# First down projection of a two-block kernel: each product as two of 64 rows into two banks

## What is computed

```python
def conv_ffn(x, g_norm, w_up, conv_k, conv_b, w_down):
    h = rms_norm(x, g_norm)
    up = h @ w_up
    ...
    gate, val = jnp.split(up, 2, axis=-1)
    return x + (jax.nn.silu(gate) * val) @ w_down
```

## Time and profile before

| | |
|---|---|
| Median of three runs | 2355.01 us (2355.0 to 2355.7) |
| Span of the profiled execution | 2353.4 us |
| What the runs' median has beside the profiled span | 1.6 us |
| TensorE busy | 2343.1 us, 12,183 products and as many weight loads |
| VectorE busy | 1516.3 us |
| ScalarE busy | 1223.8 us |
| DMA | 432.66 MB, mean 184 GB/s |
| Mean granted TensorE clock | 1.000 |

### The profile page before, as it was taken

The page is one execution under the profiler, slowest core; times in us unless marked ns, Lnnn a source line. Parts: engine busy times, 40 slices in busy tenths (PEclk is TensorE's granted clock), DMA queues, the critical chain, the costliest instruction groups (busy, mean ns, idle before and its releaser), DMA issues.

```text
span 2353.4 us, 35087 instructions
## 1 busy us (share of the span) xinstructions
PE 2343.1 (100%) x12183; PEld 1963.4 (83%) x12183; DVE 1516.3 (64%) x2146; ACT 1223.8 (52%) x1931; POOL 68.7 (3%) x92
## 2 busy tenths in 40 slices
PE   9999999999999999999999999999999999999999
PEld 7887788888888888888888878888887888888887
DVE  5657655556577775477776668787876755555554
ACT  5445544444465554355554475756465455555543
POOL 0011200000200000000000000000000000000000
PEclk9999999999999999999999999999999999999999
DMA  8665555565656656566655655555554575656555
GB/s 272 219 207 178 171 190 190 180 200 185 222 179 196 193 183 199 182 196 188 194 184 189 192 154 169 153 169 151 161 149 148 180 223 163 193 155 187 169 169 171
DMA packets 289497, 432.66 MB, mean 184 GB/s; under 512 B 32976, under 2 KB 129136, under 8 KB 289264
## 3 DMA queue, kind: packets, MB, share of 16 engines
q1 hardware_dynamic: 282976, 422.69, 57.6%
q10 hardware_dynamic: 6416, 8.56, 1.1%
HBM read 429.07 MB, written 7.10 MB: 185 GB/s over the span
## 4 chain that ended last, share of the span: by engine, by line
PE 95%; DVE 2%; ACT 1%; DVEq 1%; issue 0%; DMA 0%; ACTq 0%
PE gemm L559 22%; PE gemm L561 22%; PE gemm L560 22%; PE gemm L544 7%; PE aux L544 7%; PE gemm L537 3%; PE aux L537 3%; PE aux L1939 2%; DVE w_lo L504 1%; PE aux L561 1%; PE aux L560 1%; PE aux L559 1%; ACT w_hi L494 1%; PE aux L2180 0%; PE aux L2399 0%; PE aux L2380 0%
## 5 line engine op out<-in xcount | busy, mean ns | idle before, releaser
L504 DVE TENSOR_TENSOR w_lo<-raw,w_hi 128x1024 fp32r<-128x1024 f32 (+1 forms) x800 | 958.1, 1206 | 572.3 <-ACT w_hi L494 567.4
L494 ACT ACTIVATE w_hi<-raw 128x1024 fp32r<-128x1024 f32 (+1 forms) x800 | 815.6, 1042 | 506.0 <-PE gemm L561 402.7
L559 PE MATMUL gemm<-w_lo,hT 128*128 128x512 f32 x1600 | 637.0, 398 | 0.7 <-DVE hT L1224 0.6
L561 PE MATMUL gemm<-w_hi,hT 128*128 128x512 f32 x1600 | 624.0, 390 | 0.0
L560 PE MATMUL gemm<-w_hi,hT 128*128 128x512 f32 x1600 | 623.3, 390 | 0.0
L559 PEld LDWEIGHTS gemm<-w_lo,hT 128*128 128x128 f32 x1600 | 300.6, 188 | 64.8 <-issue 4.1
L561 PEld LDWEIGHTS gemm<-w_hi,hT 128*128 128x128 f32 x1600 | 300.3, 188 | 63.8
L560 PEld LDWEIGHTS gemm<-w_hi,hT 128*128 128x128 f32 x1600 | 300.8, 188 | 58.8 <-issue 0.2
L544 PE MATMUL gemm<-hT,w_hi 128*128 128x512 f32 x704 | 218.5, 393 | 0.1
L544 PE MATMUL aux<-hT,w_hi 128*128 128x512 f32 x672 | 208.0, 390 | 0.0
L559 PE MATMUL gemm<-w_lo,yT_hi 128*128 128x512 f32 x472 | 184.3, 390 | 0.5 <-DVE yT_lo L1467 0.5
(11 more groups left out here) (341 smaller groups left out, 2283.4 us busy)
## 6 DMA issues: line engine op xcount, KB each, us to landing
raw<-in_w_up SPq DMA_DIRECT2D x336, 256.0 KB, 2.9
raw<-in_w_in SPq DMA_DIRECT2D x144, 512.0 KB, 4.4
raw<-in_a_w_in SPq DMA_DIRECT2D x128, 512.0 KB, 3.6
raw<-in_b_w_in SPq DMA_DIRECT2D x128, 512.0 KB, 4.2
raw<-in_w_down SPq DMA_DIRECT2D x76, 512.0 KB, 4.6
raw<-in_w_branch SPq DMA_DIRECT2D x32, 512.0 KB, 4.5
raw<-in_w_out SPq DMA_DIRECT2D x32, 512.0 KB, 4.7
raw<-in_a_w_out SPq DMA_DIRECT2D x32, 512.0 KB, 3.7
```

What stands on the lines that cost most here:

```text
L494: nc.scalar.activation(hi, src, ACT.Copy).then_inc(S("hi_done"), 1)
L504: nc.vector.tensor_tensor(lo, src, hi.bitcast(F32), ALU.subtract).then_inc(S("lo_done"), 1)
L559: nc.tensor.matmul(dst, xh, wl[:, k, :], start=h["start"] and k == 0, stop=False)
L561: mm = nc.tensor.matmul(dst, xl, wh[:, k, :], start=False, stop=h["stop"] and k == h["n"] - 1)
```

## The change

For tiles 41 to 44, each of the three products of a k block and token block is done as two: the lower 64 rows of both operands into the tile's `G` bank, the upper 64 rows into the `AX` bank with the number `t % 2 * 2 + tb`. Both banks hold half of the sum over the rows. The three terms now stand in one loop, each with its two halves. At the end of such a tile VectorE first adds the `AX` bank to `x`, drains, and then adds the `G` bank; the signal to TensorE comes from the second. All other tiles are as before.

```diff
--- before.py
+++ after.py
@@ -508,6 +508,14 @@
 
             return T_UP1 <= t < T_DOWN1 or T_UP2 <= t < T_DOWN2
 
+        def in_row_halves(t):
+
+            return T_DOWN1 <= t < T_UP2
+
+        def half_banks(t, tb):
+
+            return G[t % 2][tb], AX[t % 2 * 2 + tb]
+
         def up_banks(t):
 
             return G[t % 2] + AX[t % 2 * 2:t % 2 * 2 + 2]
@@ -552,7 +560,16 @@
             order = [(k, tb) for k in range(h["n"]) for tb in range(TB)]
             if t == N_TILES - 1 and h["stop"]:
                 order.sort(key=lambda at: at[1])
-            for k, tb in () if is_up(t) else order:
+            if in_row_halves(t):
+                for k, tb in order:
+                    at = slice(tb * P, (tb + 1) * P)
+                    terms = ((hi, wl), (hi, wh), (lo, wh))
+                    for i, (xs, ws) in enumerate(terms):
+                        for rows_, dst in zip((slice(0, C), slice(C, P)), half_banks(t, tb)):
+                            mm = nc.tensor.matmul(dst[:, 0:w], xs[rows_, h["kt"] + k, at], ws[rows_, k, :],
+                                                  start=h["start"] and k == 0 and i == 0,
+                                                  stop=h["stop"] and k == h["n"] - 1 and i == 2)
+            for k, tb in () if is_up(t) or in_row_halves(t) else order:
                 xh = hi[:, h["kt"] + k, tb * P:(tb + 1) * P]
                 xl = lo[:, h["kt"] + k, tb * P:(tb + 1) * P]
                 dst = (AX[tb] if t in IN_AUX else G[t % 2][tb])[:, 0:w]
@@ -1423,6 +1440,9 @@
                 for tb in range(TB):
                     dst = x[:, tb, bass.ds(at, 512)]
                     src = AX[tb] if t in IN_AUX else G[t % 2][tb]
+                    if in_row_halves(t):
+                        V.tensor_tensor(dst, dst, half_banks(t, tb)[1][:, :], ALU.add)
+                        dve.drain()
                     V.tensor_tensor(dst, dst, src[:, :], ALU.add).then_inc(S(f"read_out{tb}"), 1)
 
             run(half, 8, turn_merged(3))
```

## The result

The change takes 2360.72 us (median of 11 runs, 2359.81 to 2361.11) against 2355.15 for the kernel before (11 runs): a ratio of 1.0023, 95% interval 1.0015 to 1.0031. That is 5.6 us slower; 2360.9 was predicted, 5.9 over before.

What follows compares the result with a forecast made beforehand. TensorE's stream was taken to bound the kernel, with VectorE costing only where TensorE waits. Joints 5.5, mode changes 0.4 and products 0 gave 5.9 us over the median 2355.0: 2360.9, range 2355.5 to 2366.5.

Steps and rivals of the forecast that it cites:

- The adds at the joints: Between a tile's end and the third half's w_lo, VectorE's doubled adds cost 1.52 us at each of three places, 4.56 us.
- The products: In the first down projection, each pair of 64-row products costs what one undivided product did, 226.7 ns: 0 added.
- the fp32 pace: Rival for the divided products: pairs run at 0.216 us each, -5.6 us, giving 2355.8, no change; chance 0.20.
- the whole product's pace: For the divided products: 226.7 ns per pair, as for one undivided fp32r product of 512 columns.
- The remainder of fp32r: About 13 ns beyond streaming in each fp32r product; forecast: a pair pays it together; the fp32 pace has it vanish.
- The second start: Rival: each pair of divided products pays 0.01 us for its second product's start, 5.3 us, giving 2365.7; chance 0.12.
- Entering and leaving: TensorE's one switch into 64-row mode costs 0.19 us and the one out 0.20, together 0.4.
- The fourth joint: After the last divided tile, at the second up projection's first tile, the adds cost 0.99 us after slack.
- Nothing else queues behind the adds: On VectorE after the adds: raw tile loads follow w_lo, issued four halves ahead; the bank's next writer is two tiles away.
- The sum: Over the whole kernel: 5.5 + 0.4 + 0 = 5.9 us, added to the median 2355.0: 2360.9, or 0.25% more.
- The likeliest case: The forecast itself for the whole kernel, 2360.9 us, reaching from 2359.7 to 2362.3 with its unknown adds; chance 0.55.

Runs made afterwards that it cites:

- adds-only run: Kernel before, with each bank of the first down projection added twice to x, a drain between, and products undivided: 2360.16 us, ratio 1.0021.
- third half first: VectorE splits the next tile's third weight half before waiting for the tile's end: 2354.39 us on the change, 2354.74 on the kernel before.
- pairs-only run: The change without the second add, so products are divided but VectorE adds only the gemm bank: 2355.74 us, ratio 1.0004 to the kernel before.
- the runs with many changes: The change for token block 0 only: 2393.06 us; the same with each half's products sorted by token block: 2376.41 us.
- third half first with the products of before: Kernel before, with VectorE splitting the next tile's third weight half before it waits for the tile's end: 2354.74 us, ratio 0.9998.
- halves far apart: The change, with all lower-row products of a half of the weights before all upper-row ones: 2475.59 and 2443.45 us in two runs.

## Why the prediction was right

*The adds at the joints: right.* Forecast 1.52 at each of three, by two adds and two drains; measured 4.6 us in all in the waits, and 1.57 a tile with the slower restart. The mechanism is shown twice: the adds-only run alone loses 5.0, and with the third half first it is all gone. Only the form was other than said: the chain has no product of 1.8 us, it leaves TensorE and goes through the adds.

*The products: right, for 0.* The choice between the fp32 pace and the whole product's pace fell to the second, and the pairs run every 0.23 us like the products of the earlier trace rows. The remainder of fp32r stays when two products share the array. Had it gone, the pairs-only run would have been 4 to 5 us below before and not 0.6 above. The second start is not paid: the two of a pair start 0.00 to 0.01 us apart, and the next pair is not later for it. The Trainium skill's rule was that each further tile of a pack adds some 4 ns (the Trainium skill, "TensorE: Matmul & The Clock Gate", section "Measured speedup vs the span model"). Across this stream of pairs that does not add up: by an estimate from this figure it would be 2.1 us, and the pairs-only run loses 0.5 in the whole stage, with both changes of mode.

*Entering and leaving: right*, 0.4. In the runs with many changes it is 0.43 to 0.44 for there and back.

*The fourth joint: right for the adds by themselves, too high for the change.* Forecast 0.99, and 0.20 beside it for leaving the mode. How late TensorE is against the kernel before can be read from the starts of the same products ahead of this joint (988.95 before) and behind it (990.35 before). With the adds alone they are 994.66 and 997.04: from 5.71 to 6.69, so 0.98, as forecast. In the change they are 994.19 and 996.37: from 5.24 to 6.02, so 0.78. Leaving the mode has made TensorE 0.2 later already, and that much less is left to wait for. The forecast added two terms that overlap.

"Nothing else queues behind the adds" is not borne out either. Later, at 1004.8, TensorE waits again. Before, there was a stall at the same place:

```profile
998.51 0.30 PEld L544 LDWEIGHTS gemm<-hT,w_hi 128*128 128x128 f32 x2 [0.48 <-issue]
```

and after:

```profile
1002.36 1.06 ACT L494 ACTIVATE w_hi<-raw 128x1024 fp32r<-128x1024 f32 x1 [1.87 <-DMA raw<-in_w_up]
...
1004.79 0.30 PEld L552 LDWEIGHTS gemm<-hT,w_hi 128*128 128x128 f32 x2 [0.74 <-issue]
```

At the head of the second up tile w_lo is late because w_hi waited for the load of the raw tile (1.87 us, the row at 1002.36), and that load may start only when w_lo has freed the raw tile. The chain of the change runs this way, from the adds by w_lo, SyncE and the load to the product at 1004.82: a delay of VectorE can come back by way of SyncE four halves later. Here it is 0.26 us more than before. But VectorE's delay alone does not set it. The adds-only run has the same adds and waits only 0.2 us at this place, and the pairs-only run, whose joints are the old ones, does not wait there at all; nor do the two runs with the third half first. What else decides, the time of the load perhaps, stays open.

*The sum: the number owes something to luck.* By the starts of the same products in the two profiled executions the change is 0.12 us late ahead of the stage (866.82 against 866.70), 5.24 behind it, 6.02 behind the fourth joint and 6.27 behind the stall at 1004.8 (1005.82 against 999.55). So the stage and its tail cost 6.15, not the 5.9 of the forecast: three times 1.57 and 0.4 for the mode, then 0.78 and 0.26. The spans differ by only 5.6, because two later stalls, far behind the change, are shorter in it by 0.37 us each. The first of them, before:

```profile
1236.02 0.69 DVE L1462 TENSOR_TENSOR conv_val<-conv_gate,conv_val 128x512 f32<-128x512 f32 x1 [0.46 <-issue]
...
1240.24 0.19 PEld L559 LDWEIGHTS gemm<-w_lo,yT_hi 128*128 128x128 f32 x1 [0.90 <-DVE yT_lo L1467]
```

and after:

```profile
1241.92 0.69 DVE L1482 TENSOR_TENSOR conv_val<-conv_gate,conv_val 128x512 f32<-128x512 f32 x1
...
1246.14 0.19 PEld L576 LDWEIGHTS gemm<-w_lo,yT_hi 128*128 128x128 f32 x1 [0.53 <-DVE yT_lo L1487]
```

Before, VectorE stands still for 0.46 us and waits for nothing that the profile shows; after, it does not, and TensorE is stopped for 0.37 us less. The second place is at 1757.83 us before (VectorE, 0.46 again) and 1773.66 (TensorE). The three kernels whose VectorE has 2146 instructions (before, pairs only, third half first with the products of before) have both gaps; the other seven, with 2150 or 2154, have neither. So this goes with the number of VectorE's instructions, and not with the pairs or with the order; why is open. In the profiled execution of the change with the third half first it makes up 0.7 of the 1.1 us by which that span lies below the one before.

*The range and the chances.* The likeliest case came, and 5.6 us is just past the 4.7 us from which I had counted slower. The range of 2355.5 to 2366.5 also held most of the fp32 pace and the second start, so the number alone would not have told these cases apart; the experiments do.

## What to carry to other kernels

Dividing a product over the rows gives nothing to an engine whose rows were full: two of 64 rows run side by side in the time of one of 128, and the price is a second bank to read. Before adding work to the engine that prepares the next operands, look at the tile's end: an engine with a third of its time free can still have no slack where it stands still for a signal and has its next piece behind it. Moving one piece of preparation ahead of that wait cost three lines here and gave back all 6 us. And keep kinds of tiling together: each change of mode cost 0.2 us.

## What was not expected of the hardware

- TensorE takes products of the other row half forward past those that wait, out of program order. With three in a series nothing is lost (2360.52 against 2360.72 us). With twelve in a series a product of the other half passes the last three at most, and a half of the weights takes 3.91 us instead of 2.72.
- The granted clock can fall to half while TensorE is busy without a gap: 0.50 from about 917 to 987 us in the run with the halves far apart, beginning some 2 us behind a wait of 1.3 us. Such a tile takes 76 us instead of 43 to 44.
- A change between 128-row and 64-row products is not hidden in a running stream: 0.09 us at the change and 0.11 at the step after it, each way.
- Where VectorE had four or eight more instructions in the first down projection, two gaps of 0.46 us on VectorE, 250 and 770 us later, were gone, and TensorE's stalls behind them were some 0.25 to 0.37 us shorter. So a difference of a few tenths of a microsecond between two of these kernels can come from a place that the change does not touch.
